# Order of the heads' steps, causal presets and last evictions in a two-layer hybrid decoder kernel on one Trainium2 core

## The chip, the cores and the metric

One core of a Trainium2 chip (trn2) runs the whole program. The metric is the device time of one execution in microseconds; the figure for a kernel is the median over its runs.

## The reference, cut to what matters

The input is 256 real tokens of 1024 float32 features; 16 learned meta tokens stand before them. Two layers are computed, each with three sublayers on the residual stream h:

```python
h = h + 0.5 * swiglu(rmsnorm(h, ffn1_norm[l]), ffn1_w_gu[l], ffn1_w_down[l])
h = h + mixer(rmsnorm(h, mix_norm[l]), ...)
h = h + 0.5 * swiglu(rmsnorm(h, ffn2_norm[l]), ffn2_w_gu[l], ffn2_w_down[l])
...
return rmsnorm(h, final_norm)[:, CHUNK:]
```

The mixer projects u to queries, keys, values and gates at once and runs two branches of 8 heads. Branch A is retention: decayed causal scores times values, then a group norm per head (mean and variance over 128 features) and a swish gate. Branch B is stick-breaking attention: with z the scaled, strictly causal scores, log(1 - sigmoid(z)) is summed over the keys behind each key, and the weights are exp of log sigmoid(z) plus that sum:

```python
log_1mb = jnp.where(mask, jax.nn.log_sigmoid(-z), 0.0)
acc = lax.cumsum(log_1mb, axis=3, reverse=True) - log_1mb
a = jnp.where(mask, jnp.exp(jax.nn.log_sigmoid(z) + acc), 0.0)
```

Both branches are projected to 1024 features, gated, added and projected once more.

## The kernel before

**Layout and weights.** Features lie on the 128 partitions and tokens along the free axis: 272 (16 meta and 256 real), in the last layer's mixer 256 wherever only real tokens are still needed. All weights come as one stream of pieces of 128 x 1024 float32, each one step of the program: 66 steps in each feed-forward part and 72 in each mixer, 408 in all. Sync's queue loads a piece into one of four slots of raw. To keep float32 accuracy with the fast format, ScalarE rounds it (split_hi, w_hi), VectorE subtracts (split_lo, w_lo = raw - w_hi), and TensorE multiplies each of a piece's 8 blocks three times: hi by hi, hi by lo, lo by hi (use, L1176 to L1178), 24 matmuls a piece. Step s on ScalarE and VectorE prepares the piece of step s + 4, in the slot that TensorE's piece s has just left; its load waits on lo_ready in Sync's queue.

**The mixer's steps.** mixer(l) exists once for each engine, as a loop over step s, and the order of the statements in each loop is the order of that engine's queue. TensorE's order in a step is: the piece, with a head's subtract_sums before its fourth block on odd steps from 39 on; then retention's and stick-breaking's small matmuls. Retention's head hd begins at step RET0 + 2 hd = 24 + 2 hd, stick-breaking's head hd at SB0 + 2 hd = 37 + 2 hd, so that retention's heads 6 and 7 and stick-breaking's heads 0 and 1 share steps 37 to 41.

**Retention, a head.** Scores (L1332), decay on VectorE (dec, L1074 and L1075), output on TensorE in bank 5 (L1424); then ScalarE makes ro, its square rs and the rounded square rs_hi (L567 to L569), VectorE the remainder rs_lo (L886, semaphore rs_split), and at the end of the next step TensorE sums both over the features (the variance, L1431 and L1432, which wait for rs_split). ScalarE takes ln and exp (L574, L576), VectorE scales and gates (L872, L875), ScalarE rounds (L563), VectorE subtracts (L880).

**Stick-breaking, a head.** TensorE writes the scores to bank 6 (L1332). Heads 0 to 2 (hd < KEPT_MASKS) get the causal mask by one more matmul (L1477), identity by minus 2 to the 100th. For heads 3 to 7 ScalarE has written the mask into the bank beforehand (z_mask, L606, semaphore z_masked) and the scores are added to it. ScalarE then makes ln(1 + exp(-|z|)) in three activations on sa (Abs L581, Exp L583, Ln L585; sa is the view ssq in the trace). VectorE adds a correction for the short last keys (L905), makes the softplus sp twice, whole and rounded (L909), and the remainder sp_lo (L912, semaphore sp_ready). TensorE subtracts the running sums (subtract_sums, L1321 and L1322, semaphore cum_done), ScalarE takes the exponential (L597; heads 4 to 7 a rounded second one, pa_hi, with its remainder pa_lo on VectorE, L900), and TensorE multiplies by the values in bank 7 (L1462 or L1457). VectorE adds the last queries' part (L1015), ScalarE rounds the output (rounded_output, L502), VectorE subtracts (L917, semaphore sb_ready). In heads 0 to 3 rounded_output stands ahead of the exponential in ScalarE's loop, in heads 4 to 7 behind the preset.

In the trace the names on the left of an arrow are those of the buffers: sa is ssq, sp is sqh, rs and rr are gv, rs_hi and sp_hi lie in gh, rs_lo and sp_lo in gl, out_tok in rv_gb.

**The end.** After the last feed-forward part TensorE sums each token's squares (L1517) and transposes the gained features into banks 0 to 3 (turn_rows, L1297): first halves of both token blocks ahead of the last blocks of weights, second halves behind the sums. VectorE computes the mean square (ms, L1109), ScalarE the root (L685), VectorE the reciprocal (L1111). Then VectorE scales the first halves out of PSUM (L1115) and ScalarE the second halves (L689), 512 columns each, and four DMAs store the output: three on Sync's queue (L347, L349, L351), one on ScalarE's (L691).

## Time and profile before

| | |
|---|---|
| median of 3 runs | 1289.11 us (1289.01 to 1289.24) |
| profiled execution | 1289.24 us |
| its span | 1287.4 us |
| TensorE busy | 1279.5 us, 99% of the span |
| VectorE busy | 875.7 us, 68% |
| ScalarE busy | 703.6 us, 55% |
| GpSimd busy | 55.6 us, 4% |
| read from HBM | 217.04 MB, 169 GB/s over the span |
| chain that ended last, on TensorE | 98% of the span |

The span is the time from the first to the last instruction on the core; the profiled execution's own time holds it and what lies around it. Busy time of TensorE is the union of its matmuls' records, and a record lasts longer than the distance to the next matmul's start, because matmuls are pipelined. L numbers are lines of the kernel before; engines are called PE (TensorE), PEld (its weight loads), DVE (VectorE), ACT (ScalarE), POOL (GpSimd) and SP (Sync).

### The profile page before, as it was taken

The page shows a single profiled execution, that of the slowest core. Times are in us where ns is not written, and L with a number is a line of the kernel's source. Part 1 is how long each engine was busy: PE and PEld are TensorE (multiplying, and loading weights), DVE is VectorE, ACT ScalarE, POOL GpSimd, SP SyncE. Part 2 cuts the span into 40 slices and gives each one's busy share as a digit, 9 for nine tenths or more (in the row PEclk, how much of TensorE's full clock was granted, in tenths as well). Part 3 has the DMA queues.
Part 4 walks back from the last instruction along what each step waited for, and adds up shares of the span by engine and source line. Part 5 has one row for each costly group of instructions (what it writes and reads, how often), then busy time and mean ns, then how long its engine had stood idle before and what let it go on. Part 6 is the DMA issues. An engine that isn't in the chain of part 4 may idle for free.

```text
span 1287.4 us, 26188 instructions
## 1 busy us (share of the span) xinstructions
PE 1279.5 (99%) x10302; PEld 1274.4 (99%) x10302; DVE 875.7 (68%) x1103; ACT 703.6 (55%) x955; POOL 55.6 (4%) x48
## 2 busy tenths in 40 slices
PE   9999999999999999999999999999999999999998
PEld 8999999999999999999999999999999999999998
DVE  7766556878777776665576665568788877766653
ACT  6444446757777554444454444467678775544442
POOL 2000001000000010000010000010000000100000
PEclk9999999999999999999999999999999999999999
DMA  7655554554344555555545555545543445655552
GB/s 295 211 173 171 179 178 150 190 168 135 126 137 147 167 179 178 172 177 174 180 159 185 179 173 173 178 164 180 176 136 132 146 152 178 197 188 183 184 180 82
DMA packets 60705, 219.30 MB, mean 170 GB/s; under 512 B 6864, under 2 KB 6992, under 8 KB 60496
## 3 DMA queue, kind: packets, MB, share of 16 engines
q1 hardware_dynamic: 60192, 217.27, 50.8%
q8 instruction: 63, 1.03, 0.3%
q10 hardware_dynamic: 432, 0.85, 0.2%
q14 instruction: 18, 0.15, 0.0%
HBM read 217.04 MB, written 1.05 MB: 169 GB/s over the span
## 4 chain that ended last, share of the span: by engine, by line
PE 98%; DVE 1%; ACT 1%; DMA 0%; issue 0%; DVEq 0%; ACTq 0%
PE bank L1176 31%; PE bank L1178 31%; PE bank L1177 31%; PE bank L1332 1%; PE bank L1424 1%; PE bank L1321 1%; PE bank L1304 0%; PE bank L1462 0%; DMA raw<-stream 0%; PE bank L1457 0%; PE bank L1339 0%; PE bank L1131 0%; DVE w_lo L698 0%; PE bank L1322 0%; PE bank L1135 0%; PE bank L1133 0%
## 5 line engine op out<-in xcount | busy, mean ns | idle before, releaser
L698 DVE TENSOR_TENSOR w_lo<-raw,w_hi 128x1024 fp32r<-128x1024 f32 x407 | 510.6, 1261 | 262.5 <-ACT w_hi L423 257.3
L1176 PE MATMUL bank<-xh,w_hi 128*128 128x272 f32 (+1 forms) x2224 | 641.2, 288 | 0.0
L423 ACT ACTIVATE w_hi<-raw 128x1024 fp32r<-128x1024 f32 x407 | 427.8, 1057 | 381.4 <-PE bank L1178 380.4
L1178 PE MATMUL bank<-xh,w_lo 128*128 128x272 f32 (+1 forms) x2224 | 635.9, 286 | 0.0
L1177 PE MATMUL bank<-xl,w_hi 128*128 128x272 f32 (+1 forms) x2224 | 635.5, 286 | 0.0
L1177 PEld LDWEIGHTS bank<-xl,w_hi 128*128 128x128 f32 x2224 | 418.6, 188 | 0.0
L1176 PEld LDWEIGHTS bank<-xh,w_hi 128*128 128x128 f32 x2224 | 418.3, 188 | 0.0
L1178 PEld LDWEIGHTS bank<-xh,w_lo 128*128 128x128 f32 x2224 | 418.0, 188 | 0.0
L1178 PE MATMUL bank<-gh,w_lo 128*128 128x272 f32 (+1 forms) x1016 | 290.9, 286 | 0.0
L1176 PE MATMUL bank<-gh,w_hi 128*128 128x272 f32 (+1 forms) x1016 | 290.5, 286 | 0.0
L1177 PE MATMUL bank<-gl,w_hi 128*128 128x272 f32 (+1 forms) x1016 | 289.7, 285 | 0.0
L1177 PEld LDWEIGHTS bank<-gl,w_hi 128*128 128x128 f32 x1016 | 191.4, 188 | 0.0
L1178 PEld LDWEIGHTS bank<-gh,w_lo 128*128 128x128 f32 x1016 | 191.0, 188 | 0.0
L1176 PEld LDWEIGHTS bank<-gh,w_hi 128*128 128x128 f32 x1016 | 191.0, 188 | 0.0
L472 ACT ACTIVATE gh<-gv 128x544 f32 (+3 forms) x44 | 28.7, 652 | 89.2 <-DVE gv L787 89.2
L367 POOL TENSOR_TENSOR ssq<-ssq,sqh 128x544 f32<-128x544 f32 x17 | 27.8, 1635 | 977.6 <-ACT sqh L437 977.6
L789 DVE TENSOR_TENSOR gl<-gv,gh 128x544 f32 (+3 forms) x44 | 31.6, 717 | 41.3 <-ACT gh L472 41.3
L779 DVE TENSOR_TENSOR gv<-bank,act 128x544 f32<-128x544 f32 (+1 forms) x44 | 31.5, 716 | 22.5 <-PE bank L1178 22.5
L428 ACT ACTIVATE xh<-gain_h 128x272 fp32r<-128x272 f32 (+1 forms) x48 | 22.2, 512 | 42.9 <-DVE gain_h L727 42.9
L772 DVE TENSOR_TENSOR scl<-bank,r 128x544 f32<-128x544 f32 (+1 forms) x44 | 31.4, 714 | 1.5
L787 DVE TENSOR_TENSOR gv<-gv,r 128x544 f32<-128x544 f32 (+1 forms) x44 | 31.3, 710 | 0.1
L468 ACT ACTIVATE act<-scl 128x544 f32<-128x544 f32 (+1 forms) x44 | 28.1, 638 | 5.9 <-DVE scl L772 5.9
(213 smaller groups left out, 750.2 us busy)
## 6 DMA issues: line engine op xcount, KB each, us to landing
raw<-stream SPq DMA_DIRECT2D x407, 512.0 KB, 3.3
table<-tables SPq DMA_DIRECT2D x1, 1424.0 KB, 8.7
out<-rv_gb SPq DMA_DIRECT2D x3, 256.0 KB, 2.6
gain_h<-tokens SPq DMA_DIRECT2D x2, 272.0 KB, 6.4
raw<-stream SPq DMA_DIRECT2D x2, 256.0 KB, 4.5
rv_gb<-squares SPq DMA_DIRECT2D x1, 384.0 KB, 8.2
gain_h<-tokens ACTq DMA_DIRECT2D x1, 300.0 KB, 4.3
gain_h<-tokens ACTq DMA_DIRECT2D x1, 272.0 KB, 5.2
```

What stands on the lines that cost most here:

```text
L367: pool.tensor_tensor(ssq[:, :, :], ssq[:, :, :], squares_home(rnd, p), ALU.add).then_inc(ssq_added, 1)
L423: eng.activation(w_hi[:, slot, :], raw[:, slot, :], ACT.Copy).then_inc(hi_ready, 1)
L468: eng.activation(act[:, :, q0:T], scl[:, :, q0:T], ACT.Silu).then_inc(gate_act, 1)
L472: eng.activation(gh[:, bass.ds(it * 2, 2), q0:T], gv[:, :, q0:T], ACT.Copy).then_inc(gh_ready, 1)
L698: eng.tensor_tensor(w_lo[:, slot, :], raw[:, slot, :], w_hi[:, slot, :].bitcast(F32), ALU.subtract).then_inc(lo_ready, 1)
L772: eng.tensor_tensor(scl[:, :, q0:T], pair(b, q0), twice(r, q0), ALU.mult).then_inc(gate_scaled, 1)
L779: eng.tensor_tensor(gv[:, :, q0:T], pair(b + 2, q0), act[:, :, q0:T], ALU.mult).then_inc(up_gated, 1)
L787: eng.tensor_tensor(gv[:, :, q0:T], gv[:, :, q0:T], twice(r, q0), ALU.mult).then_inc(g_val, 1)
L789: eng.tensor_tensor(gl[:, bass.ds(it * 2, 2), q0:T], gv[:, :, q0:T], gh[:, bass.ds(it * 2, 2), q0:T].bitcast(F32), ALU.subtract).then_inc( ...
L1176: pe.matmul(out, wh, hi, start=first, stop=False)
L1177: pe.matmul(out, wh, lo, start=False, stop=False)
L1178: mm = pe.matmul(out, wl, hi, start=False, stop=last)
```

## The change

Five things change, none in what is computed.

- KEPT_MASKS goes from 3 to 1: heads 1 and 2 get the mask as a preset too, and lose the mask matmul.
- In ScalarE's loop the three activations of the softplus move ahead of ro, rs and rs_hi (steps 37 and 39). In VectorE's loop rs_lo moves behind the softplus chain.
- On the odd steps of LATE_HI (43 to 51) ScalarE's split_hi runs behind those three activations; split_lo of the steps of LATE_LO (43 to 53) runs one step later, behind the softplus chain.
- rounded_output of heads 0 to 3 moves behind the exponential and the preset.
- At the end VectorE copies both first halves out of PSUM unscaled before it waits for the sums, and scales them in place afterwards; the last two chunks of the second token block are transposed into bank 5 and scaled by VectorE, so that ScalarE's second eviction has 256 columns; the stores of Sync's queue change places and ScalarE's store waits for VectorE's part too.

```diff
--- before.py
+++ after.py
@@ -77,12 +77,14 @@
 K_HI, K_HI_TURNED = [(10, 12), (26, 28)], [(11, 13), (30, 32)]
 K_LO, K_LO_TURNED = [(14, 16), (28, 30)], [(16, 18), (36, 38)]
 Q_HI, Q_LO = [(14, 15), (34, 40)], [(18, 20), (36, 42)]
+LATE_HI = range(SB0 + 6, SB0 + 2 * HEADS, 2)
+LATE_LO = range(SB0 + 6, SB0 + 2 * HEADS + 1, 2)
 NEG = -2.0 ** 100
 GAINS = (3 * DEPTH + 1) * DC
 HALF = PIECE // 2
 WARM = 5
 STACKED = HEADS // 2
-KEPT_MASKS = 3
+KEPT_MASKS = 1
 OUT_TOK = [N_META, N_META + P]
 
 
...
@@ -345,10 +347,10 @@
                     load(j, i * RING + j)
             sp_.wait_ge(out_ready, 1)
             sp_.dma_start(h_out[0:P, 0:4 * P], out_tok[:, 0, 0:4 * P]).then_inc(out_stored, 16)
+            sp_.wait_ge(out_ready, 2)
+            sp_.dma_start(h_out[P:2 * P, 0:4 * P], out_tok[:, 1, 0:4 * P]).then_inc(out_stored, 16)
             sp_.wait_ge(out_halves, 1)
             sp_.dma_start(h_out[0:P, 4 * P:], out_tok[:, 0, 4 * P:]).then_inc(out_stored, 16)
-            sp_.wait_ge(out_ready, 2)
-            sp_.dma_start(h_out[P:2 * P, 0:4 * P], out_tok[:, 1, 0:4 * P]).then_inc(out_stored, 16)
             sp_.wait_ge(out_stored, 16 * 4)
 
         @block.gpsimd
@@ -507,7 +509,8 @@
                 for s in range(MIX):
                     if s >= S_OUT and s % 2:
                         take_h(l * 3 + 2, (s - S_OUT) // 2, qf)
-                    split_hi(base + (s + RING), (FFN + s) % RING)
+                    if s not in LATE_HI:
+                        split_hi(base + (s + RING), (FFN + s) % RING)
                     u = s // 2
                     if s == 1:
                         squares_hi(l * 3 + 1, 0)
@@ -561,6 +564,16 @@
                     if (s - RET0) % 2 == 1 and 0 <= hd < HEADS:
                         eng.wait_ge(gated, l * HEADS + (hd + 1))
                         eng.activation(gh[:, RET_C + hd, qf:T], rn[:, qf:T], ACT.Copy).then_inc(rh_ready, 1)
+                    hd = (s - SB0) // 2
+                    if (s - SB0) % 2 == 0 and 0 <= hd < HEADS:
+                        eng.wait_ge(z_done, l * HEADS + (hd + 1))
+                        eng.activation(sa[:, qf:], bank[:, 6, qf:SCORES], ACT.Abs).then_inc(sa_step, 1)
+                        eng.wait_ge(sa_step, l * 3 * HEADS + (3 * hd + 1))
+                        eng.activation(sa[:, qf:], sa[:, qf:], ACT.Exp, scale=-1.0).then_inc(sa_step, 1)
+                        eng.wait_ge(sa_step, l * 3 * HEADS + (3 * hd + 2))
+                        eng.activation(sa[:, qf:], sa[:, qf:], ACT.Ln, bias=1.0).then_inc(sa_step, 1)
+                        if s in LATE_HI:
+                            split_hi(base + (s + RING), (FFN + s) % RING)
                     hd = (s - RET0 - 1) // 2
                     if (s - RET0) % 2 == 1 and 0 <= hd < HEADS:
                         eng.wait_ge(ret_o_joined, l * HEADS + (hd + 1))
@@ -575,19 +588,9 @@
                         eng.wait_ge(ln_ready, l * HEADS + (hd + 1))
                         eng.activation(rr[:, qf:T], rr[:, qf:T], ACT.Exp, scale=-0.5).then_inc(rr_ready, 1)
 
-                    hd = (s - SB0) // 2
-                    if (s - SB0) % 2 == 0 and 0 <= hd < HEADS:
-                        eng.wait_ge(z_done, l * HEADS + (hd + 1))
-                        eng.activation(sa[:, qf:], bank[:, 6, qf:SCORES], ACT.Abs).then_inc(sa_step, 1)
-                        eng.wait_ge(sa_step, l * 3 * HEADS + (3 * hd + 1))
-                        eng.activation(sa[:, qf:], sa[:, qf:], ACT.Exp, scale=-1.0).then_inc(sa_step, 1)
-                        eng.wait_ge(sa_step, l * 3 * HEADS + (3 * hd + 2))
-                        eng.activation(sa[:, qf:], sa[:, qf:], ACT.Ln, bias=1.0).then_inc(sa_step, 1)
                     hd = (s - SB0 - 3) // 2
                     if (s - SB0) % 2 == 1 and 0 <= hd < HEADS:
-                        if hd < STACKED:
-                            rounded_output(l, hd, qf)
-                        else:
+                        if hd >= STACKED:
                             f0 = DK * (hd % 2)
                             eng.wait_ge(sbo_done, l * HEADS + (hd + 1))
                             eng.activation(so_low[f0:f0 + DK, qf:T], bank[DK - f0:2 * DK - f0, 7, qf:T], ACT.Copy).then_inc(so_low_ready, 1)
@@ -605,7 +608,7 @@
                                 eng.wait_ge(pa_hi_ready, l * STACKED + (hd - STACKED + 1))
                             eng.activation(bank[:, 6, qf:SCORES], z_mask[:, qf:], ACT.Copy).then_inc(z_masked, 1)
                     hd = (s - SB0 - 3) // 2
-                    if (s - SB0) % 2 == 1 and STACKED <= hd < HEADS:
+                    if (s - SB0) % 2 == 1 and 0 <= hd < HEADS:
                         rounded_output(l, hd, qf)
 
                     k = s - (SB0 + 2 * HEADS)
@@ -683,11 +686,12 @@
             layers(layer)
             eng.wait_ge(tok_ms, 1)
             eng.activation(r[:, 0:2], ms[:, 0:2], ACT.Sqrt).then_inc(tok_rms, 1)
-            for i in range(2):
+            for i, c1 in enumerate((DC * P, 6 * P)):
                 eng.wait_ge(tok_r, 1)
                 eng.wait_ge(turned, 3 + i)
-                eng.activation(out_tok[:, i, 4 * P:], bank[:, 2 * i + 1, :], ACT.Copy, scale=ms[:, i:i + 1]).then_inc(out_halves, 1)
+                eng.activation(out_tok[:, i, 4 * P:c1], bank[:, 2 * i + 1, 0:c1 - 4 * P], ACT.Copy, scale=ms[:, i:i + 1]).then_inc(out_halves, 1)
             eng.wait_ge(out_halves, 2)
+            eng.wait_ge(out_ready, 3)
             eng.dma_start(h_out[P:2 * P, 4 * P:], out_tok[:, 1, 4 * P:]).then_inc(out_stored, 16)
 
         @block.vector
@@ -879,11 +883,6 @@
                         eng.wait_ge(rh_ready, l * HEADS + (hd + 1))
                         eng.tensor_tensor(gl[:, RET_C + hd, qf:T], rn[:, qf:T], gh[:, RET_C + hd, qf:T].bitcast(F32),
                                           ALU.subtract).then_inc(ret_ready, 1)
-                    hd = (s - RET0 - 2) // 2
-                    if (s - RET0) % 2 == 0 and 0 <= hd < HEADS:
-
-                        eng.wait_ge(rs_ready, l * 2 * HEADS + 2 * (hd + 1))
-                        eng.tensor_tensor(rs_lo[:, qf:T], rs[:, qf:T], rs_hi[:, qf:T].bitcast(F32), ALU.subtract).then_inc(rs_split, 1)
                     if s == SB_TAIL + 1:
                         eng.wait_ge(sa_tail_step, 3 * l + 3)
                         for whole_or_hi in (sp_tail, sp_tail_hi):
@@ -910,6 +909,13 @@
                                                      ALU.max, ALU.add).then_inc(sp_made, 1)
                         eng.wait_ge(sp_made, l * 2 * HEADS + 2 * (hd + 1))
                         eng.tensor_tensor(sp_lo[:, qf:], sp[:, qf:], sp_hi[:, qf:].bitcast(F32), ALU.subtract).then_inc(sp_ready, 1)
+                    if s - 1 in LATE_LO:
+                        split_lo(base + (s - 1 + RING), (FFN + s - 1) % RING)
+                    hd = (s - RET0 - 2) // 2
+                    if (s - RET0) % 2 == 0 and 0 <= hd < HEADS:
+
+                        eng.wait_ge(rs_ready, l * 2 * HEADS + 2 * (hd + 1))
+                        eng.tensor_tensor(rs_lo[:, qf:T], rs[:, qf:T], rs_hi[:, qf:T].bitcast(F32), ALU.subtract).then_inc(rs_split, 1)
                     hd = (s - SB0 - 4) // 2
                     if (s - SB0) % 2 == 0 and 0 <= hd < HEADS:
                         eng.wait_ge(sbh_ready, l * HEADS + (hd + 1))
@@ -1032,7 +1038,8 @@
                                                       ALU.subtract).then_inc(q_ready, 1)
 
                     for n in [] if s == MIX - 2 else [s - 1, s] if s == MIX - 1 else [s]:
-                        split_lo(base + (n + RING), (FFN + n) % RING)
+                        if n not in LATE_LO:
+                            split_lo(base + (n + RING), (FFN + n) % RING)
 
                     hd = (s - SB0 - 3) // 2
                     if (s - SB0) % 2 == 1 and STACKED <= hd < HEADS:
@@ -1105,14 +1112,19 @@
             split_lo(3, 3)
             layers(layer)
 
+            for i in range(2):
+                eng.wait_ge(turned, 1 + i)
+                eng.tensor_copy(out_tok[:, i, 0:4 * P], bank[:, 2 * i, :]).then_inc(out_moved, 1)
             eng.wait_ge(sums_done, 1)
             eng.tensor_scalar(ms[:, 0:2], bank[:, 4, 0:2], 1.0 / DC, EPS, ALU.mult, ALU.add).then_inc(tok_ms, 1)
             eng.wait_ge(tok_rms, 1)
             eng.reciprocal(ms[:, 0:2], r[:, 0:2]).then_inc(tok_r, 1)
+            eng.wait_ge(tok_r, 1)
+            eng.wait_ge(out_moved, 2)
             for i in range(2):
-                eng.wait_ge(tok_r, 1)
-                eng.wait_ge(turned, 1 + i)
-                eng.tensor_scalar(out_tok[:, i, 0:4 * P], bank[:, 2 * i, :], ms[:, i:i + 1], None, ALU.mult).then_inc(out_ready, 1)
+                eng.tensor_scalar(out_tok[:, i, 0:4 * P], out_tok[:, i, 0:4 * P], ms[:, i:i + 1], None, ALU.mult).then_inc(out_ready, 1)
+            eng.wait_ge(turned, 4)
+            eng.tensor_scalar(out_tok[:, 1, 6 * P:], bank[:, 5, 0:2 * P], ms[:, 1:2], None, ALU.mult).then_inc(out_ready, 1)
 
         @block.tensor
         def _(pe):
@@ -1294,7 +1306,8 @@
 
                 pe.wait_ge(gained, 4 * half + 4)
                 for c in range(4 * half, 4 * half + 4):
-                    mm = pe.transpose(bank[:, 2 * i + half, P * (c % 4):P * (c % 4) + P], hg[:, c, P * i:P * i + P], ident)
+                    b, k = (5, c - 6) if i and c > 5 else (2 * i + half, c % 4)
+                    mm = pe.transpose(bank[:, b, P * k:P * k + P], hg[:, c, P * i:P * i + P], ident)
                 mm.then_inc(turned, 1)
 
             def turn_values(b, cols):
```

**ScalarE, step 37 of layer 0** (w_hi of step 37; then retention's heads 5 and 6 and stick-breaking's head 0). Before:

```order
L423 ACTIVATE w_hi<-raw 128x1024 [waits raw_ready3,piece_done]
L563 ACTIVATE gh<-xg 128x272 [waits gated]
L567 ACTIVATE ro<-bank 128x272 [waits ret_o_joined]
L568 ACTIVATE gv<-bank 128x272
L569 ACTIVATE gh<-bank 128x272
L581 ACTIVATE ssq<-bank 128x416 [waits z_done]
L583 ACTIVATE ssq<-ssq 128x416 [waits sa_step]
L585 ACTIVATE ssq<-ssq 128x416 [waits sa_step]
```

and now:

```order
L425 ACTIVATE w_hi<-raw 128x1024 [waits raw_ready3,piece_done]
L566 ACTIVATE gh<-xg 128x272 [waits gated]
L570 ACTIVATE ssq<-bank 128x416 [waits z_done]
L572 ACTIVATE ssq<-ssq 128x416 [waits sa_step]
L574 ACTIVATE ssq<-ssq 128x416 [waits sa_step]
L580 ACTIVATE ro<-bank 128x272 [waits ret_o_joined]
L581 ACTIVATE gv<-bank 128x272
L582 ACTIVATE gh<-bank 128x272
```

The three activations on ssq (Abs, Exp, Ln) have gone ahead of ro, gv (rs) and gh (rs_hi); step 39 changes alike.

**VectorE, step 38 of layer 0** (retention's head 6, stick-breaking's head 0). Before:

```order
L880 TENSOR_TENSOR gl<-xg,gh 128x272 [waits rh_ready]
L886 TENSOR_TENSOR gl<-gv,gh 128x272 [waits rs_ready]
L895 COPY sums_tail<-bank 32x128 [waits cum_tail_done]
L905 TENSOR_TENSOR ssq<-ssq,sums_tail 32x16 [waits sa_step,sums_tail_ready]
L909 SCALAR_TENSOR_TENSOR sqh<-bank,ssq 128x416 [waits sa_joined]
L909 SCALAR_TENSOR_TENSOR gh<-bank,ssq 128x416
L912 TENSOR_TENSOR gl<-sqh,gh 128x416 [waits sp_made]
L698 TENSOR_TENSOR w_lo<-raw,w_hi 128x1024 [waits hi_ready,piece_done]
```

and now:

```order
L884 TENSOR_TENSOR gl<-xg,gh 128x272 [waits rh_ready]
L894 COPY sums_tail<-bank 32x128 [waits cum_tail_done]
L904 TENSOR_TENSOR ssq<-ssq,sums_tail 32x16 [waits sa_step,sums_tail_ready]
L908 SCALAR_TENSOR_TENSOR sqh<-bank,ssq 128x416 [waits sa_joined]
L908 SCALAR_TENSOR_TENSOR gh<-bank,ssq 128x416
L911 TENSOR_TENSOR gl<-sqh,gh 128x416 [waits sp_made]
L918 TENSOR_TENSOR gl<-gv,gh 128x272 [waits rs_ready]
L702 TENSOR_TENSOR w_lo<-raw,w_hi 128x1024 [waits hi_ready,piece_done]
```

rs_lo (gl<-gv,gh, which waits for rs_ready) has moved from the second place to behind sp_lo (gl<-sqh,gh).

**TensorE, the end of step 38 and the start of step 39 in layer 0**, now:

```order
L1444 MATMUL bank<-gh,square_r 128x272 [waits rs_split]
L1445 MATMUL bank<-gl,square_r 128x272
L1345 MATMUL bank<-qs,gh 128x272
L1345 MATMUL bank<-qs,gl 128x272
L1345 MATMUL bank<-qs,gh 128x144
L1345 MATMUL bank<-qs,gl 128x144
L1188 MATMUL bank<-xh,w_hi 128x272 [waits lo_ready]
```

The two matmuls of the variance still stand ahead of the piece whose fourth block waits for sp_ready; nothing moved here.

**ScalarE, steps 40 and 41 of layer 0** (retention's head 7, stick-breaking's heads 0 to 2), now:

```order
L425 ACTIVATE w_hi<-raw 128x1024 [waits raw_ready2,piece_done]
L587 ACTIVATE gv<-bank,eps 128x272 [waits ret_var]
L589 ACTIVATE gv<-gv 128x272 [waits ln_ready]
L600 ACTIVATE xg<-bank 128x416 [waits cum_done]
L609 ACTIVATE bank<-z_mask 128x416 [waits pa_ready]
L504 ACTIVATE gh<-bank 64x272 [waits sbo_joined]
L653 ACTIVATE qs<-rk 64x2x272 [waits ret_scores,unit_evicted]
L653 ACTIVATE qs<-rk 64x2x272
L425 ACTIVATE w_hi<-raw 128x1024 [waits raw_ready3,piece_done]
L566 ACTIVATE gh<-xg 128x272 [waits gated]
L570 ACTIVATE ssq<-bank 128x416 [waits z_done]
L572 ACTIVATE ssq<-ssq 128x416 [waits sa_step]
```

Before, the row gh<-bank 64x272 stood ahead of xg<-bank, and there was no row bank<-z_mask.

## Rows read from the trace of the kernel before

**Rows 1.** The page, part 1: busy time, share, instructions.

```profile
PE 1279.5 (99%) x10302; PEld 1274.4 (99%) x10302; DVE 875.7 (68%) x1103; ACT 703.6 (55%) x955; POOL 55.6 (4%) x48
```

**Rows 2.** Timeline of PE, layer 1: start us, length us, engine, line, operation.

```profile
991.94 0.28 PE L1177 MATMUL bank<-xl,w_hi 128*128 128x256 f32 x1
992.06 0.28 PE L1178 MATMUL bank<-xh,w_lo 128*128 128x256 f32 x1
992.44 0.45 PE L1321 MATMUL bank<-gh,square_r 128*128 128x400 f32 x1
```

**Rows 3.** Waits of the whole span: us in total, times, longest.

```profile
PEld bank L1321 <- DVE gl L912: 1.1, 5, 0.3
...
PEld bank L1457 <- DVE gl L900: 0.5, 2, 0.3
```

**Rows 4.** Timeline of PE, layer 0: the mask matmul of head 2.

```profile
353.63 0.33 PE L1477 MATMUL bank<-square_r 128*128 128x256 f32 x1
353.80 0.29 PE L1176 MATMUL bank<-xh,w_hi 128*128 128x272 f32 x1
```

**Rows 5.** Timeline, layer 0, around head 2's sums; brackets: idle before, releaser.

```profile
353.40 1.06 ACT L423 ACTIVATE w_hi<-raw 128x1024 fp32r<-128x1024 f32 x1 [0.18 <-PE bank L1178]
...
357.72 0.59 DVE L912 TENSOR_TENSOR gl<-sqh,gh 128x416 fp32r<-128x416 f32 x1
...
358.57 0.39 ACT L502 ACTIVATE gh<-bank 64x272 fp32r<-64x272 f32 x1 [0.52 <-DVE bank L1015]
...
358.63 0.35 PE L1321 MATMUL bank<-gh,square_r 128*128 128x416 f32 x1
...
360.00 0.52 ACT L606 ACTIVATE bank<-z_mask 128x416 f32<-128x416 f32 x1
```

**Rows 6.** Timeline, layer 0, steps 37 and 38: retention's head 6, stick-breaking's head 0.

```profile
336.34 0.38 ACT L567 ACTIVATE ro<-bank 128x272 f32<-128x272 f32 x1
...
337.17 0.53 ACT L581 ACTIVATE ssq<-bank 128x416 f32<-128x416 f32 x1
...
337.64 0.43 DVE L886 TENSOR_TENSOR gl<-gv,gh 128x272 fp32r<-128x272 f32 x1
...
339.51 0.29 PE L1431 MATMUL bank<-gh,square_r 128*128 128x272 f32 x1
...
340.30 0.59 DVE L912 TENSOR_TENSOR gl<-sqh,gh 128x416 fp32r<-128x416 f32 x1
```

**Rows 7.** Timeline, the same two instructions at layer 0's head 7 and layer 1's heads.

```profile
346.07 0.39 ACT L567 ACTIVATE ro<-bank 128x272 f32<-128x272 f32 x1
...
348.38 0.29 PE L1431 MATMUL bank<-gh,square_r 128*128 128x272 f32 x1
...
978.90 0.37 ACT L567 ACTIVATE ro<-bank 128x256 f32<-128x256 f32 x1
...
981.76 0.28 PE L1431 MATMUL bank<-gh,square_r 128*128 128x256 f32 x1
...
988.03 0.38 ACT L567 ACTIVATE ro<-bank 128x256 f32<-128x256 f32 x1
...
990.20 0.28 PE L1431 MATMUL bank<-gh,square_r 128*128 128x256 f32 x1
```

**Rows 8.** Timeline of the end, from the last gain to the last store's issue.

```profile
1280.42 0.35 DVE L738 TENSOR_SCALAR rg<-gain_h 128x256 f32<-128x256 f32 x1
...
1281.54 0.16 DVE L1109 TENSOR_SCALAR ms<-bank 128x2 f32<-128x2 f32 x1 [0.76 <-PE bank L1517]
...
1282.16 1.41 DVE L1115 TENSOR_SCALAR rv_gb<-bank,ms 128x512 f32<-128x512 f32 x2
...
1283.81 0.44 SPq L351 DMA_DIRECT2D out<-rv_gb  x1
```

**Rows 9.** Groups by form, DVE: count | busy us, mean ns | idle us before.

```profile
L756 DVE CAST square_r<-rv_gb 128x768 fp32r<-128x768 f32 x1 | 0.6, 556 | 0.0
```

**Rows 10.** Windows before the first pieces: stretch, length, busy by engine, clock, DMA.

```profile
5.20:6.50 1.30, 0.38 (x2) 0.01 (x1) 0.91 (x2) 1.30 (x4) 0.00 (x0) 1.00 1.04 421
```

2 lines of the change are left out of this document (1 added, 1 removed).

## The prediction

> **What bounds the kernel now.** I read the page first. TensorE is busy through the whole span [rows 1], so a microsecond counts only where TensorE itself starts late; the rest of VectorE and ScalarE is cover. A matmul's record runs on past the start of the next, so a busy share cannot show a small wait. I therefore read the timeline of PE from start to start: inside a piece of weights (a step of 24 matmuls, about 3 us) the distance is 0.12 us, and before the first matmul of subtract_sums in head 1 of layer 1 it is 0.38 us, so TensorE stood for 0.26 us there [rows 2]. The view of waits says that VectorE's sp_lo (L912) held up five such places by 1.1 us in all, and pa_lo (L900) two places by 0.5 us [rows 3]. These 1.6 us are what earlier softplus chains can give back. Last I laid the durations of the trace on the new order of each engine, for steps 37 to 43 of both mixers, where retention's last heads and stick-breaking's first heads overlap.
>
> **The change part by part.**
>
> Mask matmuls. Heads 1 and 2 lose L1477 in both layers, four matmuls. From its start to the next matmul's start lie 0.17 us [rows 4], so 4 x 0.17 = 0.68 us, all on TensorE's path; the lower bound is the 0.12 us of a matmul inside a piece, 0.48 us. The row is the operation itself, so I take it. The Trainium skill's page "TensorE: Matmul & The Clock Gate", part "Wait, 56ns, not 53.3ns?", puts matmuls in a stream at their columns over 2.4 GHz plus 2.5 ns. By that four of 256 columns are worth 0.44 us; the row shows more.
>
> Presets. Heads 1 and 2 now wait for z_masked, so ScalarE writes their preset (0.52 us each, four added) behind the exponential of the head before. That is in time: head 3 always had one, it ended at 360.52, and TensorE still had five eighths of a piece (15 x 0.12 = 1.9 us) behind the sums that began at 358.63 [rows 5]. It delays what stands behind it on ScalarE, which is counted under head 2.
>
> Softplus chain ahead of retention's rounding (steps 37 and 39). On ScalarE Abs, Exp and Ln of a stick-breaking head now run ahead of ro, rs and rs_hi of a retention head (L567 to L569), so Abs starts where L567 started. On VectorE rs_lo (L886) moves behind ssq, sp, sp_hi and sp_lo. But TensorE needs rs_lo first: the matmuls of the variance (L1431) stand at the end of the same step, ahead of the next step's subtract_sums, and they have not moved. This term decides. From the start of Abs to the end of sp_lo lie 340.30 + 0.59 - 337.17 = 3.72 us; rs_lo adds 0.43 us [rows 6]; successive instructions overlap by some 0.1 us: 4.05 us from the start of Abs to the end of rs_lo. Against the old start of L1431:
> layer 0, head 0: 336.34 + 4.05 - 339.51 = 0.88 us late [rows 6];
> layer 0, head 1: 346.07 + 4.05 - 348.38 = 1.74 us [rows 7];
> layer 1, head 0: 978.90 + 4.05 - 981.76 = 1.19 us [rows 7];
> layer 1, head 1: 988.03 + 4.05 - 990.20 = 1.88 us [rows 7].
> The sum is 5.7 us of standing TensorE. Nothing hides it: TensorE takes its queue in order, and the scores of the next head and every later piece wait behind L1431 though their weights are ready. Lower bound 4.5 us (the other engines catch up while TensorE stands), upper bound 6.5 us.
>
> Head 2. In step 40 ScalarE now writes head 2's preset (0.52 us) and, moved behind it, head 0's rounded output (0.39 us, formerly done before the sums came), then both halves of qs, then w_hi, and only then, in step 41, head 2's Abs, because w_hi is put off only from step 43 on. That w_hi had 0.18 us of idle time ahead of it. So the chain of head 2 comes 0.91 - 0.18 = 0.73 us later; its sp_lo ended at 357.72 + 0.59 = 358.31, 0.32 us before the sums at 358.63 [rows 5], and TensorE arrives 0.17 us earlier for want of the mask matmul. 0.73 - 0.32 + 0.17 = 0.58 us, in two layers about 1.1 us; bounds 0 (what the stops before it give the other engines) and 1.6 us.
>
> w_hi and w_lo behind the chains of heads 3 to 7. A w_hi and a w_lo leave the chain's way. That takes away the 1.6 us of [rows 3]: head 1's share, since the stop at L1431 covers it, and the last head's pa_lo, which now goes ahead of a w_lo. Bounds 1.0 and 1.9 us. It costs nothing: a w_lo is put off by one step at most, and it is for the piece four steps on, some 9 us before TensorE reads it. The load that waits for it on SP's queue starts a step later too and still lands before its w_hi is due. If that cover were gone, TensorE would wait for whole w_hi and w_lo times.
>
> The tail. VectorE is free at 1280.42 + 0.35 = 1280.77 us, and the sums arrived at 1281.54 [rows 8]. Two copies out of PSUM now come first. Two scaled evictions of their size took 1.41 us [rows 8], so the copies end at about 1282.15 and ms starts 0.6 us late; root and reciprocal follow as before, and the scaling starts at 1282.76 instead of 1282.16. It is now in place, from SBUF: 256 columns took 0.35 us [rows 8] and 768 columns of a cast 0.56 us [rows 9], so 512 take about 0.45, twice, and the last 256 columns out of PSUM 0.4: VectorE ends at about 1284.1. The last two outputs are then issued at about 1284.1, where the last one was issued at 1283.81. I take 0.3 us slower; bounds -0.1 (the copies take half as long) and +0.7 us. The Trainium skill's page "VectorE: DVE Perf Modes", part on the TRN2 errata, makes such an operation 58 cycles plus half the columns at 0.96 GHz, 0.33 us for 512 columns; by it the tail would be about level with before. For 256 columns it says 0.19 us where the row has 0.35, so the row decides.
>
> **Sum.** -0.68 + 5.7 + 1.1 - 1.6 + 0.3 = +4.8 us. The profiled execution took 1289.24 us (its span is 1287.4), 0.13 us over the median of 1289.11; taken from the median, the changed kernel comes to 1293.9 us.
>
> **The rivals.**
>
> A. The early chains win, and rs_lo is in time, because ScalarE and VectorE reach it sooner than I lay it out. For it: L1431 started 1.4 us after the old end of rs_lo in layer 0, head 0 [rows 6], and the chain starts 0.8 us earlier. Against it: rs_lo has the whole chain of 3.72 us ahead of it, and starting that 0.8 us earlier cannot make it fit. Without the stops and head 2's: -0.68 - 1.6 + 0.3 = -2.0 us, 1287.1 us, chance 0.11; with a tail at its lower bound and waits at their upper one -2.7 us, 1286.4 us, chance 0.04.
>
> B. The first stop of each layer comes, but the two engines catch up during it, so that the second is 1 us and head 2's is nil: 0.88 + 1.0 + 1.19 + 1.0 = 4.1 us, the sum +2.1 us, 1291.2 us. For it: ScalarE and VectorE have idle time in every step. Against it: the second chain starts from TensorE's own scores, and so moves with TensorE. Chance 0.10.
>
> C. The stops lower TensorE's granted clock. For it only their length. Against it: TensorE did next to nothing for 1.3 us before the first pieces, and the granted clock stayed at 1.00, the level of 2.4 GHz [rows 10]; a stop here is up to 1.9 us. The Trainium skill's page "TensorE: Matmul & The Clock Gate", part "What's actually happening", has an idle engine fall to 1.2 GHz. One piece at half the clock behind each of four stops costs 4 x 3 = 12 us more, 1306 us. Chance 0.03.
>
> D. Heads 3 to 7 do not get what the change says: their chains start earlier, but TensorE waits for a late w_lo or load. Against it is the distance of four steps. One microsecond in each of five heads and two layers gives 1304 us. Chance 0.02.
>
> **How the numbers follow.** The forecast has 0.70, A 0.15, B 0.10, C 0.03, D 0.02. The forecast's bounds (4.5 to 6.5 for the stops, 0 to 1.6 for head 2, 1.0 to 1.9 for the waits, -0.1 to 0.7 for the tail), not all at one end together, give +2.7 to +6.7 us, 1291.8 to 1295.8 us. The range reaches down over B: 1290.4 to 1296.0 us; A, C, D and the edges are left out, 2 in 10. A measurement of this kernel can tell 0.2%, 2.6 us, from no change. Slower by more: the forecast, half of B, C and D, 0.80. Within: half of B and A's first case, 0.16. Faster: A's second case, 0.04.
>
> **What would show it.** In PE's timeline of the changed kernel: before the variance matmuls of the last two retention heads of each layer a distance of 1 to 2 us, released by rs_lo; before head 2's subtract_sums about half a microsecond; at heads 3 to 7 nothing over 0.15 us; four matmuls fewer; ms 0.6 us further behind the last gain. If the distance before the variance matmuls stays under 0.3 us, the main step is wrong; if w_lo or a load releases any piece, the cover that I name is.

## The result, and the profile after

The changed kernel takes 1295.45 us (median of five executions, 1294.23 to 1295.80), the kernel before 1289.01 in the same session: ratio 1.0047, 95% interval 1.0035 to 1.0058, so about half a per cent slower. The forecast was 1293.9 (1290.4 to 1296.0, slower); the range holds the time, and the forecast is 1.55 us under the median. The profiled execution took 1295.52 us with a span of 1293.7.

The five times are in two groups: 1294.23 and 1294.24, then 1295.45, 1295.52 and 1295.80. That will need a cause of its own.

The page's busy line, and from the view of waits the lines that answer to [rows 3] ("engine line waited for: total us, times, longest us"). Lines have moved: the piece's matmuls are L1188 to L1190, the variance matmuls L1444 and L1445, subtract_sums begins at L1334, rs_lo is L918 and sp_lo L911.

```profile
PE 1280.9 (99%) x10298; PEld 1275.8 (99%) x10298; DVE 876.7 (68%) x1106; ACT 705.9 (55%) x959; POOL 55.6 (4%) x48
...
PEld bank L1444 <- DVE gl L918: 6.1, 4, 2.0
...
PE bank L1444 <- DVE gl L918: 5.2, 4, 1.8
...
PEld bank L1334 <- DVE gl L911: 0.9, 2, 0.6
```

The four matmuls fewer are in the count (10298 for 10302). TensorE is still busy in 99% of the span, and yet it stands four times for the remainder rs_lo (gl is its tile's name in the trace), 1.5 us a time, and twice for head 2's sp_lo. The waits of [rows 3] have gone from the list: the chains of heads 3 to 7 and the last head's pa_lo hold TensorE up no more. The largest stop, layer 1, head 1, in the timeline (start us, us, engine, line, output and inputs, count, idle time and releaser):

```profile
992.04 0.49 ACT L570 ACTIVATE ssq<-bank 128x400 f32<-128x400 f32 x1
...
993.13 0.54 ACT L574 ACTIVATE ssq<-ssq 128x400 f32<-128x400 f32 x1
...
993.84 0.38 ACT L581 ACTIVATE gv<-bank 128x256 f32<-128x256 f32 x1
...
993.88 0.28 PE L1190 MATMUL bank<-xh,w_lo 128*128 128x256 f32 x1
...
994.11 0.39 ACT L582 ACTIVATE gh<-bank 128x256 fp32r<-128x256 f32 x1
...
995.00 0.58 DVE L911 TENSOR_TENSOR gl<-sqh,gh 128x400 fp32r<-128x400 f32 x1
...
995.50 0.42 DVE L918 TENSOR_TENSOR gl<-gv,gh 128x256 fp32r<-128x256 f32 x1
...
995.97 0.39 PE L1444 MATMUL bank<-gh,square_r 128*128 128x256 f32 x1 [1.81 <-DVE gl L918]
996.19 0.29 PE L1445 MATMUL bank<-gl,square_r 128*128 128x256 f32 x1
```

From the start of Abs (992.04) to the end of rs_lo (995.92) lie 3.88 us; my 4.05 was close. rs_hi was ready at 994.50, and rs_lo then waited another microsecond behind sp_lo. The distance of TensorE's starts is 995.97 - 993.88 = 2.09 us where 0.12 is the rule, a stop of 1.97. The four stops measure 0.92, 1.82, 1.16 and 1.97 us, 5.87 in all. This measure leaves something out: the next matmul (L1445) starts 0.22 us behind, and the same pair lies 0.11 us apart in the kernel before. That 0.11 us more is there behind each of the four stops, so that they cost TensorE 6.3 us.

What came behind this stop I had given 3 chances in 100. Two stretches of TensorE's timeline, then the table by stretches (PEclk is the granted clock):

```profile
997.35 0.41 PE L1188 MATMUL bank<-xh,w_hi 128*128 128x256 f32 x1
997.57 0.42 PE L1189 MATMUL bank<-xl,w_hi 128*128 128x256 f32 x1
997.78 0.41 PE L1190 MATMUL bank<-xh,w_lo 128*128 128x256 f32 x1
...
1000.77 0.29 PE L1190 MATMUL bank<-xh,w_lo 128*128 128x256 f32 x1
1000.90 0.28 PE L1188 MATMUL bank<-xh,w_hi 128*128 128x256 f32 x1
```

```profile
core 0: us, PE busy (x) PEld busy (x) DVE busy (x) ACT busy (x) POOL busy (x), PEclk, DMA share, GB/s
...
996.00:997.50 1.50, 1.50 (x10) 1.45 (x11) 0.21 (x2) 0.89 (x2) 0.00 (x0) 0.94 0.05 14
997.50:1000.00 2.50, 2.50 (x13) 2.49 (x12) 1.91 (x3) 0.13 (x1) 0.00 (x0) 0.50 0.14 25
1000.00:1003.00 3.00, 3.00 (x24) 3.00 (x24) 1.11 (x2) 2.92 (x6) 0.00 (x0) 0.88 0.39 154
```

TensorE is fully busy in all of 997.50:1000.00 and starts only 13 matmuls. The granted clock is 0.50, the level of 1.2 GHz; starts of matmuls of 256 columns are 0.21 us apart, and from 1000.77 on 0.12 again. It fell after a stop of 1.97 us, about 1.4 us after TensorE had begun again, and stayed low for some 3.4 us. The busy share is 100% in the slow and in the fast stretch; only counts and starts tell them apart.

The end of the program, the answer to [rows 8] (TensorE is 6.17 us late at the last pieces):

```profile
1286.59 0.35 DVE L742 TENSOR_SCALAR rg<-gain_h 128x256 f32<-128x256 f32 x1
1286.86 1.28 DVE L1117 COPY rv_gb<-bank 128x512 f32<-128x512 f32 x2
...
1288.05 0.15 DVE L1119 TENSOR_SCALAR ms<-bank 128x2 f32<-128x2 f32 x1
...
1288.68 0.88 DVE L1125 TENSOR_SCALAR rv_gb<-rv_gb,ms 128x512 f32<-128x512 f32 x2
...
1289.48 0.48 DVE L1127 TENSOR_SCALAR rv_gb<-bank,ms 128x256 f32<-128x256 f32 x1
...
1290.06 0.44 SPq L353 DMA_DIRECT2D out<-rv_gb  x1
```

ms starts at 1288.05 - 6.17 = 1281.88, 0.34 us later than before, and the last issue at 1283.89 against 1283.81: the new end costs 0.1 us and wins nothing.

### The profile page after: what moved, and what is told of

Its sections match the earlier page's. It is cut to its first block, busy times and chain, and to the rows that moved or that the text cites. A ratio compares the mean times of both kernels' runs of the same rounds, so it can differ in the third digit from the quotient of the medians.

```text
span 1293.7 us, 26187 instructions
## 1 busy us (share of the span) xinstructions
PE 1280.9 (99%) x10298; PEld 1275.8 (99%) x10298; DVE 876.7 (68%) x1106; ACT 705.9 (55%) x959; POOL 55.6 (4%) x48
## 4 chain that ended last, share of the span: by engine, by line
PE 95%; ACT 2%; DVE 2%; issue 0%; DMA 0%; DVEq 0%; ACTq 0%
PE bank L1188 30%; PE bank L1190 30%; PE bank L1189 30%; PE bank L1345 1%; PE bank L1437 1%; PE bank L1334 1%; PE bank L1317 0%; ACT w_hi L425 0%; PE bank L1475 0%; DMA raw<-stream 0%; ACT gh L644 0%; DVE gl L911 0%; DVE sqh L908 0%; PE bank L1470 0%; PE bank L1352 0%
## 5 line engine op out<-in xcount | busy, mean ns | idle before, releaser
L1188 PE MATMUL bank<-xh,w_hi 128*128 128x272 f32 (+1 forms) x2224 | 641.9, 289 | 0.0
L1190 PE MATMUL bank<-xh,w_lo 128*128 128x272 f32 (+1 forms) x2224 | 636.3, 286 | 0.0
L1188 PEld LDWEIGHTS bank<-xh,w_hi 128*128 128x128 f32 x2224 | 418.8, 188 | 0.1
L1190 PEld LDWEIGHTS bank<-xh,w_lo 128*128 128x128 f32 x2224 | 418.5, 188 | 0.0
L1190 PE MATMUL bank<-gh,w_lo 128*128 128x272 f32 (+1 forms) x1016 | 290.9, 286 | 0.0
L1188 PE MATMUL bank<-gh,w_hi 128*128 128x272 f32 (+1 forms) x1016 | 290.5, 286 | 0.0
L1190 PEld LDWEIGHTS bank<-gh,w_lo 128*128 128x128 f32 x1016 | 191.1, 188 | 0.0
L1188 PEld LDWEIGHTS bank<-gh,w_hi 128*128 128x128 f32 x1016 | 191.0, 188 | 0.0
```

The costliest lines, as they stand in the source:

```text
L1188: pe.matmul(out, wh, hi, start=first, stop=False)
L1190: mm = pe.matmul(out, wl, hi, start=False, stop=last)
```

## The experiments

My theory: the moved rs_lo alone makes the stops and nearly all of the loss; the other parts have the sizes of my sum. Rivals: the other parts weigh more than I gave them; only VectorE's order matters, not ScalarE's; and the upper group of times is something else than the clock. Each kernel was executed 5 or 11 times, beside the kernel before on the same chip; runs 1 to 4, 5 to 8 and 9 to 12 had a chip each, where the kernel before was at 1289.17, 1289.07 and 1289.08 us. "Stop" below is the distance of TensorE's starts less what the same pair of lines takes undisturbed.

**1. The new order of the chain and of rs_lo alone, in the kernel before.**

```diff
 # ScalarE, each step
+ Abs, Exp, Ln of a stick-breaking head
  ro, rs, rs_hi of a retention head
  root and exponential of the group norm
- Abs, Exp, Ln of a stick-breaking head
 # VectorE, each step
- rs_lo
  ssq, sp, sp_hi, sp_lo
+ rs_lo
```

> The kernel before with one part of the change alone: in steps 37 and 39 Abs, Exp and Ln run ahead of ro, rs and rs_hi on ScalarE, and rs_lo behind sp_lo on VectorE; mask matmuls, w_hi, w_lo, outputs and the end stay as they were. Theory 1 (the order of rs_lo is the whole loss): four stops of TensorE before the variance matmuls, 0.9, 1.8, 1.2 and 1.9 us, in sum 5.8 us, less the 0.5 us of waits at head 1 that they cover, plus up to 1.2 us where the granted clock falls after the last one: 1294.3 to 1295.6 us, 5.3 to 6.6 us over before. Theory 2 (the loss comes from the two presets more on ScalarE and what they push back, or from the end): within 0.5 us of before, 1289 us, no stop over 0.5 us.

Measured: 1294.52 us (1294.46 to 1294.58), ratio 1.0042 (1.0028 to 1.0055), 5.35 us over before. The stops are 0.92, 1.72, 1.16 and 1.77 us. From its view of waits:

```profile
PEld bank L1431 <- DVE gl L912: 5.8, 4, 1.8
...
PEld bank L1321 <- DVE gl L907: 0.6, 3, 0.3
...
PEld bank L1457 <- DVE gl L895: 0.5, 2, 0.3
```

This one reordering makes the loss. Five of the old waits stay (1.1 us), the three before subtract_sums and the two before the last remainder; only head 1's are gone, covered by the stops. The clock stays at 1.00, and the five times lie within 0.12 us.

**2. The changed kernel with that order undone, on both engines.**

> The changed kernel with that order undone on both engines: ro, rs, rs_hi ahead of Abs on ScalarE, rs_lo ahead of the chain on VectorE; presets, postponed w_hi and w_lo, outputs and the end as in the change. Theory 1: no stop before the variance matmuls, the clock stays at its full level, four mask matmuls fewer (-0.7 us), the waits at heads 5 to 7 gone (-1.3 us), head 2's stop of 0.3 to 0.7 us in each layer stays (+1.1 us), the end +0.1: 1288.3 us, 0.7 us below before. Theory 2: the loss stays, 1294 us or more.

Measured: 1288.98 us (1288.82 to 1289.47), ratio 0.9999 (0.9990 to 1.0008): level with before, 5.3 us under the changed kernel's lower group. No stop at the variance is left. But the rest of the change, which my sum had at -0.68 + 1.1 - 1.6 + 0.3 = -0.9 us, gains 0.2 us at most, which is within the interval. From its view of waits:

```profile
PEld bank L1334 <- DVE gl L916: 2.2, 4, 0.8
```

TensorE stands before subtract_sums in head 1 (0.24 and 0.49 us) and head 2 (0.56 and 0.74 us). So some other term was too kind, and runs 5, 6 and 7 look for it.

**3. Only VectorE's rs_lo back ahead of the softplus part; ScalarE keeps the new order.**

> The changed kernel with only VectorE's half undone: rs_lo stands ahead of the chain again, ScalarE still makes ro, rs and rs_hi behind Abs, Exp and Ln. It tells whether the early Abs alone does harm. Theory 1: rs_hi is ready 1.65 us later than before, so rs_lo ends at 339.4 where the variance matmul of the kernel before began at 339.51 (no stop at head 0), and at head 1 at 349.2 against 348.4 less 0.2, a stop of about 0.9 us; VectorE waits at rs_lo with the chain behind it, so sp_lo comes late, some 0.2 us more at each subtract_sums of heads 0 and 1. In all about 2 to 3 us over x2: 1290.3 to 1291.3 us. A rival, that VectorE's order is the whole of it: equal to x2 within 0.5 us.

Measured: 1291.17 us (1291.09 to 1291.91), ratio 1.0016 (1.0007 to 1.0025). Between the two, as the theory had it; the rival, that VectorE's order is the whole, would have given run 2's time. Its waits:

```profile
PEld bank L1334 <- DVE gl L916: 2.2, 4, 0.8
PEld bank L1444 <- DVE gl L890: 2.0, 2, 1.1
```

At head 0 rs_lo is in time (TensorE then stands for sp_lo, 0.30 and 0.37 us); at head 1 it comes 0.85 and 1.01 us late, because ScalarE makes rs_hi only behind Abs, Exp and Ln. Taken back in this sequence, VectorE's order gives 3.1 of the 5.3 us (1294.28 - 1291.17, the former the median of run 11) and ScalarE's 2.2. ScalarE's order alone was not undone, so these are no prices of either by itself.

**4. The stops filled with matmuls that nobody reads.**

```diff
+ if hd >= HEADS - 2:
+     pe.wait_ge(unit_evicted, evicted(l, u - 1))
+     for _ in range(7 if hd == HEADS - 2 else 15):
+         pe.matmul(bank[:, unit_banks(u - 1), 0:2 * P], ident_r, square_r[:, 0:2 * P], start=True, stop=True)
  pe.wait_ge(rs_split, l * HEADS + (hd + 1))
```

> The changed kernel with matmuls added to fill the stops: ahead of the wait for rs_split, 7 matmuls of 256 columns at retention's head 6 and 15 at head 7, identity by a constant, into a bank that is free then; their result is not used. 44 matmuls of 0.12 us are 5.2 us of work. Theory 1 with the clock: they lie wholly within the stops, so the stops' length does not grow by more than 0.3 us, and the granted clock no longer falls behind layer 1's stop: in every execution like the faster ones of the change, 1294.2 us, and no spread of over 0.5 us. Without a part for the clock (the spread of the change is of another origin): 1295.4 us with the same spread. If the stops are not waits for rs_lo but lost throughput of TensorE: 5 us over the change, 1300 us.

Measured: 1294.54 us (1294.31 to 1294.67), ratio 1.0042 (1.0028 to 1.0056). TensorE in the stop of layer 1, head 1:

```profile
993.82 0.28 PE L1190 MATMUL bank<-xh,w_lo 128*128 128x256 f32 x1
993.94 1.96 PE L1446 MATMUL bank<-square_r 128*128 128x256 f32 x15
995.91 0.39 PE L1448 MATMUL bank<-gh,square_r 128*128 128x256 f32 x1
```

Fifteen matmuls fit between 993.94 and 995.91 and the variance starts when it did (995.97 in the changed kernel). 44 more matmuls in all cost at most 0.3 us (against the lower group), so the stop's length is rs_lo's alone; TensorE was free for all of it. And none of the five times lies in an upper group.

**5. The new end alone, in the kernel before.**

> The kernel before with only the end's part of the change (copies ahead of the means, scales in place, the last 256 columns in bank 5, stores in the new order). The changed kernel's trace had TensorE 6.17 us late at the last pieces and the last store's issue 6.25 us late, so if the end costs there what it costs alone, this is 1289.2 (between 1289.0 and 1289.4), with ms 0.3 us later than before, each scale 0.44 us and the last issue 0.1 us later. Rival (my prediction's term, +0.3, ms 0.6 later): 1289.4 to 1289.8. Second rival, that the rearranged stores pay once nothing else is late: 1288.6 to 1288.9.

Measured: 1289.19 us (1289.10 to 1289.27), ratio 1.0001 (0.9992 to 1.0010): 0.12 us over the kernel before, as the changed kernel's trace had said; too little to call it a loss.

**6. The postponed rounding alone (steps 43 to 53), in the kernel before.**

```diff
- split_hi(base + (s + RING), (FFN + s) % RING)
+ if s not in LATE_HI:
+     split_hi(base + (s + RING), (FFN + s) % RING)
 ...
  Abs, Exp, Ln
+ if s in LATE_HI:
+     split_hi(base + (s + RING), (FFN + s) % RING)
```

> The kernel before with only the postponed rounding: at steps 43 to 53 w_hi comes behind Abs/Exp/Ln on ScalarE and w_lo behind sp_lo on VectorE; masks, outputs, the reorder and the end as before. My prediction's term is -1.6 (bounds 1.0 to 1.9): the waits before subtract_sums and before the last remainder go and 1287.5 comes out (1287.1 to 1288.1). Rival: the recovered waits reappear in the same step before the variance matmul (rs_lo now stands behind nothing new, but Abs/Exp/Ln hold no earlier place on ScalarE than before), so little is gained: 1288.8 to 1289.3, with stops in heads 3 to 7 that only change their line.

Measured: 1287.64 us (1287.52 to 1287.71), ratio 0.9989 (0.9980 to 0.9998): 1.43 us faster. The waits in heads 3 to 7 are gone and nothing takes their place; only head 1's stops of before (0.16 and 0.27 us) remain. The rival falls.

**7. Preset masks and output roundings alone, in the kernel before.**

```diff
-KEPT_MASKS = 3
+KEPT_MASKS = 1
 ...
- if hd < STACKED:
-     rounded_output(l, hd, qf)
- else:
+ if hd >= STACKED:
 ...
- if (s - SB0) % 2 == 1 and STACKED <= hd < HEADS:
+ if (s - SB0) % 2 == 1 and 0 <= hd < HEADS:
      rounded_output(l, hd, qf)
```

> The kernel before with one kept mask instead of three and the output roundings of heads 0 to 3 behind the preset; nothing else. My prediction: four mask matmuls fewer, -0.68; at head 2 stops of about 0.58 a layer before subtract_sums, +1.1; so 1289.6 (1288.9 to 1290.0), head 1 without a stop. With the order undone in the changed kernel there were stops before subtract_sums of 0.24 and 0.49 us at head 1 and of 0.56 and 0.74 at head 2. If presets and outputs alone make them, this one shows all four, sum 2.0, and the time is 1289.11 + 2.0 - 0.7 = 1290.4; if head 1's are made by something else (the rounding postponed from step 43 on lies behind them, so it should not be), head 1 shows none and it is 1289.7.

Measured: 1290.55 us (1290.42 to 1290.63), ratio 1.0011 (1.0002 to 1.0020): 1.48 us slower. All four stops are there, 0.23 and 0.48 us at head 1, 0.55 and 0.74 at head 2. They are 2.0 us where the kernel before had 0.43 us at head 1, and TensorE loses another 0.1 us behind each of head 2's, and 0.1 us in each layer at a later head's wait. The matmuls taken away give back less than the 0.68 us of my sum. Set matmul for matmul against the kernel before, TensorE gains only 0.11 to 0.12 us at each of the four places, 0.46 us in all. Two lines show why, where head 2's mask matmul was [rows 4]:

```profile
353.41 0.34 PE L1174 MATMUL bank<-xh,w_hi 128*128 128x272 f32 x1
353.58 0.29 PE L1175 MATMUL bank<-xl,w_hi 128*128 128x272 f32 x1
```

The 0.17 us from start to start now stand behind the piece's first matmul, which took 0.12 us as long as the mask matmul was ahead of it (353.80 to 353.92). The timeline at head 2, layer 0, the answer to [rows 5]:

```profile
353.89 1.06 ACT L423 ACTIVATE w_hi<-raw 128x1024 fp32r<-128x1024 f32 x1
...
355.17 0.50 ACT L581 ACTIVATE ssq<-bank 128x416 f32<-128x416 f32 x1
...
358.18 0.29 PE L1176 MATMUL bank<-xh,w_lo 128*128 128x272 f32 x1
358.20 0.59 DVE L910 TENSOR_TENSOR gl<-sqh,gh 128x416 fp32r<-128x416 f32 x1
...
358.85 0.46 PE L1319 MATMUL bank<-gh,square_r 128*128 128x416 f32 x1 [0.39 <-DVE gl L910]
```

w_hi starts at 353.89 where it was 353.40, and sp_lo ends at 358.79 where it was 358.31: a delay of some 0.5 us from the preset and the rounded output in step 40 passes through w_hi and the whole chain. The part of the change that takes four matmuls away costs more than it gives.

**8. Old order, rounding postponed from step 41 on.** Run 2 with `LATE_HI = range(SB0 + 4, ...)`, `LATE_LO` likewise.

> The changed kernel with the old order of the chain Abs/Exp/Ln and of rs_lo on both engines (1288.98 with that alone), and the postponed rounding of w_hi and w_lo begun one head earlier, at step 41 in place of 43. Theory: head 2's stops before subtract_sums (0.56 and 0.74 us) come because w_hi of step 41 and the preset stand ahead of its Abs/Exp/Ln; with w_hi behind them they shrink by about one cast's time (0.55 us) each: 1287.9 (1287.7 to 1288.2), the first version below both kernels. Rival: VectorE's share decides (outputs' remainder and w_lo of step 40), then the stops stay over 0.4 us each and the time is 1288.8 to 1289.1.

Measured: 1287.38 us (1287.22 to 1287.47), ratio 0.9987 (0.9978 to 0.9996): faster than both kernels, 1.60 us less than run 2 (1.5 us when each is set against the kernel before on its own chip), and more than the theory's 1.1. The same place in its timeline:

```profile
354.22 0.50 ACT L576 ACTIVATE ssq<-bank 128x416 f32<-128x416 f32 x1
...
355.80 1.99 ACT L425 ACTIVATE w_hi<-raw 128x1024 fp32r<-128x1024 f32 x2
...
357.25 0.59 DVE L916 TENSOR_TENSOR gl<-sqh,gh 128x416 fp32r<-128x416 f32 x1
...
358.17 0.28 PE L1190 MATMUL bank<-xh,w_lo 128*128 128x272 f32 x1
...
358.30 0.35 PE L1334 MATMUL bank<-gh,square_r 128*128 128x416 f32 x1
```

Two w_hi run back to back behind the chain, sp_lo ends 0.46 us before TensorE asks for it, and head 2 has no stop in either layer. Head 1's stay (0.23 and 0.48 us).

**9. The same from step 39 on, and with the old end.**

> The last kernel (old order of the chain and of rs_lo, postponed rounding from step 41: 1287.38) with the rounding postponed from step 39 on, so for head 1 too, and with the end of the kernel before (the new end alone had cost 0.12). Theory: a stop before subtract_sums is there where a w_hi stands ahead of the head's Abs/Exp/Ln; head 1's two stops (0.23 and 0.48 us) then go as head 2's did: 1287.38 - 0.6 (0.1 of them stay) - 0.1 = 1286.7 (1286.5 to 1287.0). Rival: the w_hi of step 39, moved behind the chain, is late for its own piece or moves the stop to the next wait: 1287.1 to 1287.6.

Measured: 1287.34 us (1287.17 to 1287.59 and once 1288.86), ratio 0.9986 (0.9977 to 0.9995). Not 1286.7: no difference from run 8 can be told. The rule "the w_hi ahead of the chain makes the stop" fails for head 1. Its timeline there:

```profile
348.03 0.40 ACT L572 ACTIVATE gh<-bank 128x272 fp32r<-128x272 f32 x1
...
348.31 0.53 ACT L576 ACTIVATE ssq<-bank 128x416 f32<-128x416 f32 x1
...
349.92 1.99 ACT L425 ACTIVATE w_hi<-raw 128x1024 fp32r<-128x1024 f32 x2
```

What stands directly ahead of Abs there is retention's rounding (L572 is rs_hi), no w_hi, and moving that away, together with rs_lo on VectorE, is what run 1 priced at 5.35 us. Postponing w_hi past head 1's chain leaves stops of 0.30 and 0.41 us before subtract_sums, about the size of the 0.23 and 0.48 without it.

The single 1288.86 is the profiled execution, and its 1.5 us were lost at the start of the program, far from the change. The windows 6.00:10.00 of this kernel and then of run 8:

```profile
6.00:10.00 4.00, 3.37 (x15) 3.27 (x15) 3.76 (x7) 4.00 (x9) 0.00 (x0) 1.00 1.03 405
```

```profile
6.00:10.00 4.00, 3.65 (x28) 3.56 (x28) 3.77 (x8) 4.00 (x9) 0.00 (x0) 1.00 1.04 410
```

Fifteen matmuls started instead of 28, 0.23 us apart until 10.29 us and 0.12 from there on. The column says 1.00 in both, but it is not a reading here: the trace's record of the granted clock has its first entry, full clock, at 10.29 us in this execution and at 4.96 us in run 8's, and the column counts what lies ahead of the first entry as 1.00. In all fourteen traces the starts ahead of the first entry are at half the rate and those behind it at the full one (0.43 and 0.22 us for the ten opening matmuls, 0.23 and 0.12 inside a piece). In the thirteen others the entry comes at 4.9 to 7.5 us, here 2.8 to 5.4 us later, and TensorE is 1.55 us behind run 8's once the first waits for weights are over (12.05 us for 10.49). Why it came late, nothing here shows.

**10. Head 0's stops filled, head 1's empty.** The changed kernel with run 4's matmuls under `if hd == HEADS - 2:` alone.

> The changed kernel with seven extra matmuls of 256 columns, whose result nothing reads, in the wait before the variance matmul of head 0 in each layer; head 1's waits (1.82 and 1.97 us) stay empty. If the fall of the granted clock to 0.50 in layer 1 comes from head 1's stop alone, it is still there in a good part of the executions and times lie in two groups, near 1294.3 and 1295.5. If it needs both stops of a layer (1.16 us, then 1.97 us ten us later), all lie near 1294.3 with a spread under 0.5.

Measured: 1294.13, 1294.38, 1295.56, 1295.80 and 1295.88 us, ratio 1.0048 (1.0035 to 1.0062). The two groups are there although head 0's stop is gone: head 1's stop alone is enough. The profiled execution is one of the lower group, and its clock is full behind a stop of 1.98 us:

```profile
996.00:998.00 2.00, 2.00 (x17) 1.95 (x16) 0.99 (x2) 0.89 (x2) 0.00 (x0) 1.00 0.03 8
998.00:1000.00 2.00, 2.00 (x18) 2.00 (x17) 1.23 (x4) 1.45 (x4) 0.00 (x0) 1.00 0.22 61
```

**11. The changed kernel once more.**

> The changed kernel itself once more, to see how often the clock falls. The five executions so far were at 1294.23, 1294.24, 1295.45, 1295.52 and 1295.80. If the fall of the clock for some 3 us is chance in each execution, two groups 1.2 us apart come again, near 1294.3 and 1295.5, with a share of the upper between 0.3 and 0.9 in eleven; if it was something of that session, one group.

Measured: 1294.21, 1294.26, 1294.28, 1294.44 and 1295.81 us; ratio 1.0040 (1.0026 to 1.0054). Two groups again, and the one profiled here is the upper one:

```profile
996.00:998.00 2.00, 2.00 (x11) 1.95 (x11) 0.66 (x2) 0.89 (x2) 0.00 (x0) 0.64 0.03 8
998.00:1000.00 2.00, 2.00 (x11) 1.99 (x9) 1.45 (x3) 0.00 (x0) 0.00 (x0) 0.51 0.13 25
```

**12. Head 1's stops filled, head 0's empty.** Run 4's matmuls under `if hd == HEADS - 1:`.

> The changed kernel with fifteen extra matmuls of 256 columns in the wait before the variance matmul of head 1 in each layer; head 0's waits (0.92 and 1.16 us) stay empty. By every form of the clock theory the clock stays full: 1294.3 to 1294.6 in one group. If instead the upper group is made by something that the stops have nothing to do with, it shows here too, at 1295.5 to 1295.8.

Measured: 1294.37 us (1294.23 to 1294.40), ratio 1.0040 (1.0026 to 1.0054). One group.

Taken together, the upper group appeared in 4 of 10 executions of the changed kernel, in 3 of 5 with head 0's stops filled, and in none of 10 with head 1's filled (runs 4 and 12). If the filling made no difference, seven such executions of 25 would all fall among the fifteen unfilled ones about once in 75 times. Run 1, whose longest stop is 1.77 us, had none in five, on another chip than runs 10 to 12; that is too few to say that 1.77 us is short enough. Two profiles of the upper group have the clock at half for 3.4 us behind layer 1's second stop; the one profile of the lower group with the same stop has it at 1.00. The executions without a profile agree: the mean granted clock over the span is 0.997 in six of the upper group's seven and 0.998 in the other, and 0.998 or 0.999 in all eight of the lower one.

## Why the prediction held, step by step

**Mask matmuls, -0.68.** Right in kind, too large by half: in run 7 TensorE gains 0.11 to 0.12 us at each of the four places, 0.46 us in all, which is the lower bound that I gave (0.48). I took the distance behind the mask matmul itself for the gain, but what it has over 0.12 us goes over to the matmul that now stands there.

**The four stops, 5.7.** Right in place, releaser and size: 0.92, 1.82, 1.16 and 1.97 against 0.88, 1.74, 1.19 and 1.88. Adding a chain's length to the old start of its first instruction, and setting it against TensorE's old arrival, was good to 0.1 us for each. For the last one two small errors partly cancel: from the start of Abs to TensorE's start it took 3.93 us, not 4.05, and Abs came 0.21 us later, measured from TensorE's arrival, than I had it. What I left out is the slow first distance behind each stop, 0.11 us, so that TensorE lost 6.3 us, not 5.9. In time, the order is worth, less head 1's old waits, 5.35 us added to the kernel before (run 1) and 5.3 taken from the changed one (run 2).

**Presets "in time", and head 2, +1.1.** The mechanism was right at head 2, its size a little low: 0.56 and 0.74 us in run 2, and 0.66 and 0.84 us of TensorE's time with the slow distance behind them (run 7; the changed kernel's first profile shows only 0.29 for the latter stop, its second, run 11, the full 0.74). The step that failed is that the delay on ScalarE "is counted under head 2". It meets head 1 too: its stops of before, 0.16 and 0.27 us, grow to 0.24 and 0.49 in runs 2 and 7. In the changed kernel that hides under the stops at the variance. So masks and presets alone cost 1.48 us (run 7), where my two terms make 0.4.

**Waits recovered, -1.6.** Right in kind: -1.43 alone (run 6). In the changed kernel TensorE's lag falls over heads 3 to 7 from 3.06 to 2.61 us in layer 0 (359.19 to 403.32, times of before), and from 7.31 to 6.15 us in layer 1 (1000.61 to 1043.28) with the last remainder. That is 1.6 us without head 1's share, and the stops at the variance cover head 1's old waits, another 0.6 us in run 1 as TensorE's lag shows it, so that the whole is nearer 2.2. w_lo and loads release no piece, as the cover I named said.

**The end, +0.3.** Measured 0.12 (run 5). ms is only 0.34 us late, not 0.6, for three small reasons: the two copies out of PSUM took 1.28 us instead of the 1.41 of the scaled evictions, they began 0.08 us earlier than I had VectorE free (1286.86 - 6.17 = 1280.69), and ms began 0.09 us before their recorded end. The in-place scales took 0.44 us each, as estimated.

**The sum.** Run by run, alone in the kernel before: +5.35 (1), +1.48 (7), -1.43 (6), +0.12 (5), together +5.5; the lower group of the changed kernel is 5.2 over before. The parts nearly add, with 0.3 us less where head 1's stops and the variance stops cover each other. My +4.8 was 0.4 short of that, and the median is of the upper group, 1.2 us more: that is the forecast's miss of 1.55 us. That the sum came within 0.4 us is in part luck: measured by TensorE's lag, the terms are -0.46 for -0.68, 6.3 for 5.7, 1.5 for 1.1, -2.2 for -1.6 and 0.1 for 0.3, and their errors, of up to 0.6 us, largely cancel. It is luck too that the range held the upper group: it had no part for the clock.

**Rival C, the clock, 0.03.** This is where the forecast was wrong, though the range held. I argued that TensorE did nothing for 1.3 us at the start and kept its clock [rows 10], while a stop was up to 1.9 us. The row was sound: that trace's record of the clock begins at 4.89 us, ahead of it, and the piece's matmuls behind it start 0.12 us apart from the second on. But its idle time is shorter than the stop that it was set against. A stop of 1.97 us can bring the clock down. By the Trainium skill's page "TensorE: Matmul & The Clock Gate", part "What's actually happening", an idle engine falls to 1.2 GHz; two traces here agree (0.50 and 0.51), a third, with the same stop, does not (1.00). My price was wrong as well: not a piece behind each of four stops, but one place, some 3.4 us of matmuls 0.21 instead of 0.12 us apart, worth 1.2 to 1.5 us in the times. With hindsight, 7 falls in 15 executions, a chance of 0.3 to 0.5 for one such fall would have been fair, and 1.3 us for it.

Rivals A (in time) and D (late loads) are excluded by the waits. B, engines that catch up during a stop, is excluded too: the second stop of each layer is the longer.

## What to carry to other kernels

Moving a chain ahead of "less urgent" work is decided by which result TensorE asks for first in its own, unmoved order: here the remainder that was put last was needed first. Putting it, 0.43 us of VectorE's work a head, and ScalarE's steps for it behind a chain of 3.7 us cost 5.35 us over four heads. Lay the chain on the times of the old trace before such a move, count each instruction on every engine it passes, and follow a delay to all later consumers, not just the next. The piece of the change that paid was the plain one, casts that nobody needs for several steps put behind the chain; alone, with masks and order as they were, it gives 1287.64 us, and with the presets and one head more 1287.38, against 1289.07. The longer postponement without the presets, which by run 7 cost 1.48 us alone, was not run.

## What the runs showed of the hardware

The granted clock can fall to half once TensorE has stood for 1.97 us, and it doesn't do so every time: the changed kernel and run 10's, which has the same stop, gave 1294.1 to 1294.4 and 1295.5 to 1295.9 us in different executions, in 7 of 15 the latter (4 of 10 and 3 of 5). It did not in five executions with a longest stop of 1.77 us. The fall comes some time behind the stop (the first slow distance is 1.4 us after TensorE's return in the changed kernel's first trace, 1.1 us in its second), and filling the stop with unread matmuls kept the clock in ten executions of ten; it cost some 0.1 us in run 12 and at most 0.3 us in run 4. Whether the length of the stop or its place decides was not separated: layer 0's second stop, 1.8 us, was not followed by a fall in any of the traces, and no kernel made a longer one there.

Every execution that was profiled also began at half the rate. The record of the granted clock has its first entry, full clock, between 4.9 and 7.5 us, in one execution of run 9 at 10.3 us, and in all fourteen traces the starts ahead of it are at half the rate of those behind (0.23 and 0.12 us inside a piece). The column of the views shows 1.00 ahead of that entry too, so the distance of starts has to be looked at beside it.

The first distance behind a stop is longer as well: 0.22 to 0.23 us behind each of the four stops at the variance, 0.11 to 0.13 us for the same pair of matmuls in the kernel before. A short wait thus costs TensorE about 0.1 us more than it measures.
